# Router order, output products by column parity and an earlier side input in a two-layer encoder kernel

## The reference

```python
# layer 1's mixer: sliding-window attention, 16 query heads, 2 key heads, sinks
o = sliding_window_sink_attention(q, k, v, sinks)
return o @ w_out + b_out
...
# hierarchical_moe: router
g_logits = (t @ w_group) + b_group
g_prob = jax.nn.softmax(g_logits, axis=-1)
g_idx = jnp.argmax(g_logits, axis=-1)
g_w = jnp.max(g_prob, axis=-1)
e_logits = jnp.einsum('td,dge->tge', t, w_router) + b_router
e_sel = jnp.einsum('tge,tg->te', e_logits, g_onehot)
top_v, top_i = lax.top_k(e_sel, MOE_TOP_K)
top_w = jax.nn.softmax(top_v, axis=-1)
...
# every layer, at its end
gate = jax.nn.sigmoid(rms_norm(h, norm_ple[i]) @ ple_w_gate[i])
h = h + gate * (p[i] @ ple_w_proj[i])
```

## Time and profile before

| | us |
|---|---|
| median of 3 runs | 792.12 (791.20, 792.12, 795.34) |
| the profiled execution | 795.19, of which the span of the profile is 793.2 |

### The profile page before, as it was taken

The page is one execution under the profiler, slowest core; times in us unless marked ns, Lnnn a source line. Parts: engine busy times, 40 slices in busy tenths (PEclk is TensorE's granted clock), DMA queues, the critical chain, the costliest instruction groups (busy, mean ns, idle before and its releaser), DMA issues.

```text
span 793.2 us, 8335 instructions
## 1 busy us (share of the span) xinstructions
PE 747.0 (94%) x3180; PEld 346.5 (44%) x3180; DVE 278.6 (35%) x665; ACT 140.2 (18%) x344; POOL 29.9 (4%) x49
## 2 busy tenths in 40 slices
PE   6999999899999999989999979989999999988996
PEld 3445555474333333323445544476333333332444
DVE  0402331264246243323222564143533533232323
ACT  1100231222111111100311143212111111110031
POOL 0500000000000000000000020000000000000000
PEclk9999999999999999999999998989999999999999
DMA  9991521939999999999999670144999999999921
GB/s 336 325 356 55 212 88 71 391 140 358 423 421 420 421 421 421 421 421 420 385 292 299 267 299 1 53 159 164 409 421 421 422 419 421 421 421 422 404 94 54
DMA packets 49433, 245.24 MB, mean 309 GB/s; under 512 B 4080, under 2 KB 6480, under 8 KB 24816
## 3 DMA queue, kind: packets, MB, share of 16 engines
q1 hardware_dynamic: 48112, 242.15, 77.6%
q0 software_dynamic: 1104, 2.45, 0.9%
q10 hardware_dynamic: 176, 0.09, 0.0%
HBM read 243.61 MB, written 1.06 MB: 308 GB/s over the span
## 4 chain that ended last, share of the span: by engine, by line
PE 66%; DMA 15%; SPq 9%; DVE 6%; issue 3%; ACT 1%; POOLq 0%; POOL 0%; DVEq 0%; ACTq 0%
PE bank L611 28%; PE bank L849 14%; SPq L411 9%; PE bank L866 8%; DMA weights<-in_moe_w_up_dram 7%; DMA weights<-in_moe_w_down_dram 7%; PE bank L879 2%; PE bank L826 2%; PE bank L1026 1%; PE bank L595 1%; PE bank L787 1%; PE bank L858 1%; PE bank L650 1%; PE bank L670 1%; PE bank L794 1%
## 5 line engine op out<-in xcount | busy, mean ns | idle before, releaser
L611 PE MATMUL bank<-weights,normalised 128*128 128x512 f32 (+1 forms) x528 | 232.2, 594 | 10.1 <-DVE normalised L1963 4.0
L849 PE MATMUL bank<-weights,expert_rows 128*64 128x512 f32 x1024 | 228.1, 594 | 13.0 <-DMA weights<-in_moe_w_up_dram 12.9
L611 PEld LDWEIGHTS bank<-weights,normalised 128*128 128x128 f32 x528 | 100.2, 194 | 123.1 <-issue 114.5
L849 PEld LDWEIGHTS bank<-weights,expert_rows 128*64 128x64 f32 x1024 | 74.8, 137 | 155.3 <-issue 154.6
L866 PE MATMUL bank<-weights,hidden_turned 128*64 128x512 f32 x256 | 58.8, 598 | 1.3 <-DVE hidden_turned L1731 0.7
L866 PE MATMUL bank<-weights,hidden_turned_odd 128*64 128x512 f32 x256 | 58.8, 598 | 0.6 <-DMA weights<-in_moe_w_down_dram 0.6
L1317 ACT ACTIVATE gate_tanh<-bank 128x256 f32<-128x256 f32 x32 | 12.3, 385 | 206.0 <-PE bank L849 206.0
L1761 DVE TENSOR_TENSOR gather_onehots<-bank,expert_outputs 128x512 fp32r<-128x512 f32 x32 | 22.1, 691 | 54.5 <-ACT expert_outputs L1193 54.4
L1193 ACT ACTIVATE expert_outputs<-bank 128x512 fp32r<-128x512 f32 x32 | 19.1, 597 | 123.9 <-PE bank L866 123.9
L1731 DVE COPY hidden_turned<-bank 128x256 f32<-128x256 f32 x16 | 6.8, 425 | 85.1 <-PE bank L858 85.1
L1731 DVE COPY hidden_turned_odd<-bank 128x256 f32<-128x256 f32 x16 | 6.8, 425 | 78.4 <-PE bank L858 78.4
(11 more groups left out here) (249 smaller groups left out, 597.5 us busy)
## 6 DMA issues: line engine op xcount, KB each, us to landing
weights<-in_moe_w_gate_dram SPq DMA_DIRECT2D x64, 1024.0 KB, 18.6
weights<-in_moe_w_up_dram SPq DMA_DIRECT2D x64, 1024.0 KB, 20.4
weights<-in_moe_w_down_dram SPq DMA_DIRECT2D x64, 1024.0 KB, 22.3
weights<-in_even_w_in_dram SPq DMA_DIRECT2D x5, 2048.0 KB, 21.0
weights<-in_ple_w_gate_dram SPq DMA_DIRECT2D x4, 2048.0 KB, 30.9
weights<-in_even_w_out_dram SPq DMA_DIRECT2D x2, 2048.0 KB, 18.6
weights<-in_odd_w_qkv_dram SPq DMA_DIRECT2D x2, 2048.0 KB, 19.2
weights<-in_odd_w_out_dram SPq DMA_DIRECT2D x4, 1024.0 KB, 22.0
```

What stands on the lines that cost most here:

```text
L611: mm = pe.matmul(B[bank][:, 0:width], XT[:, k, tok(t)], w[:, k, :], start=(k == 0), stop=(k == KD - 1))
L849: mm = pe.matmul(bank[j * BLK:(j + 1) * BLK, :].rearrange("p (m f) -> p m f", m=2), rows[:, k, :], W[:, slots, a:a + FF // 2], start=(k == ...
```

## The change

1. On TensorE, layer 0's `experts` runs both halves of the last output product in one piece (layer 1's has one half left), and the logits of tile 0 are put on the two sides of the transposes of tile 1.
2. In the wait behind the logits, TensorE also turns `p[l]` (4 transposes to bank 3), and ScalarE copies it; `unread` goes from 12 and 9 to 10 and 8. GpSimd's queue fetches `p[l]` when layer 0's mixer inputs or layer 1's queries are turned. The work on `p` leaves the experts' steps.
3. On VectorE, the operations that lead only to the gates' weights (six behind `chosen`) move behind the gather's first copies; ScalarE's two exponentials move likewise. Two pairs of slot operations are interleaved with one wait fewer each. `rows_low(1)` is made in two parts, columns of blocks 0 to 3 ahead of the logits' wait and 4 to 7 behind the one-hots.
4. In layer 1, output products go by column parity (`out_part`): even blocks need VectorE's copy only, odd ones ScalarE's only. They begin earlier, VectorE's `mix_evac(0)` stands ahead of `max1(4)`, `turn_q(1)` ahead of `probs1(2)`, and one more half of products stands ahead of the router.
5. The bias is added to `H` by VectorE, between the updates of tile 0; GpSimd only fetches it.

The diff, cut to its core (left out: the moved SBUF buffers, the removed pieces of the experts' steps, and the same waits at other places):

```diff
+            def side_rows(l):
+
+                pool.wait_ge(*((sem("mix0_turned"), 2), (sem("q1_turned"), 4))[l])
+                pool.dma_start(PIN, p[l, 0].rearrange("(t p) d -> p t d", p=P)).then_inc(sem("p_landed"), 16)
...
             pool.tensor_tensor(BNR, BNE, HALF[:, 0:8], ALU.pow).then_inc(sem("gn_rstd"), 1)
+            side_rows(0)
             power(1)
...
             pool.dma_start(BO, bcast(odd_b_out)).then_inc(sem("bo_landed"), 16)
-            pool.wait_ge(sem("bo_landed"), 16)
-            for t in range(TT):
-                pool.wait_ge(sem("hT_ready"), 2 * (2 * 3 + t) + 2)
-                pool.wait_ge(sem("squares_ready"), 2 * 3 + t + 1)
-                pool.tensor_tensor(H[:, t, :], H[:, t, :], BO, ALU.add).then_inc(sem("bo_added"), 1)
+            side_rows(1)
...
-                for k in range(4 * half, 4 * half + 4):
+                for k in range(half, KD, 2) if n in (U_OUT1, U_OUT1 + 1) else range(4 * half, 4 * half + 4):
...
-                        pe.matmul(B[3][:, 0:P], ident, ident, start=True, stop=True)
-
-                project_rows(out, 1, 2, done)
+                        pe.matmul(B[4][:, 0:P], ident, ident, start=True, stop=True)
+
+                if l == 0:
+                    project_rows(out, 1, 2, done)
                 transposes(kn, 0, (4, 5))
-                project_part(out + 1, 1, 3, 0, done)
+                if l == 0:
+                    project_rows(out + 1, 1, 3, done)
+                else:
+                    project_part(out + 1, 1, 3, 1, done)
                 if l == 0:
                     pe.wait_ge(sem("small_landed"), 15 * 16)
                 logits(0, 0)
+                transposes(kn, 1, (6, 7))
                 logits(0, 1)
-                project_part(out + 1, 1, 3, 1, done)
-                transposes(kn, 1, (6, 7))
                 logits(1, 0)
                 logits(1, 1).then_inc(sem("logits_ready"), 1)
-                unread(12)
+                pe.wait_ge(sem("p_landed"), 16 * (l + 1))
+                pe.wait_ge(sem("h_updates"), h_done(kn - 1, 1))
+                for k in range(2):
+                    for t in range(TT):
+                        mm = pe.transpose(B[3][:, k * SEQ + t * P:k * SEQ + (t + 1) * P], PIN[:, t, k * P:(k + 1) * P], ident)
+                mm.then_inc(sem("pT_ready"), 1)
+                unread(10)
...
-                unread(9)
+                unread(8)
 
                 def gathered(group, t):
 
                     if group == 0:
                         pe.wait_ge(sem("onehots_ready"), 2 * l + t + 1)
-                        pe.wait_ge(sem("hs_low"), 2 * l + t + 1)
+                        if t == 0:
+                            pe.wait_ge(sem("pT_copied"), l + 1)
+                    if group == 0 or t == 1:
+                        pe.wait_ge(sem("hs_low"), 3 * l + 1 + t * (group + 1))
                     for k in range(4 * group, 4 * group + 4):
...
+            def out_part(c, t, bank, half):
+
+                pe.wait_ge(sem("mix1T_by_act" if half else "mix1T_by_dve"), t + 1)
+                project_part(U_OUT1 + c, t, bank, half, "out1_ready")
...
@@ -1143,29 +1148,30 @@
             probs1(1)
             scores1(3)
             values1(1)
+            turn_q(1, (6, 7))
             probs1(2)
-            turn_q(1, (6, 7))
             values1(2)
             probs1(3)
             scores1(4)
             scores1(5)
+            out_part(0, 0, 0, 0)
             values1(3)
-            mixed(0)
-            project_part(U_OUT1, 0, 0, 0, "out1_ready")
             probs1(4)
             scores1(6)
-            project_part(U_OUT1, 0, 0, 1, "out1_ready")
+            out_part(0, 0, 0, 1)
             values1(4)
             probs1(5)
             scores1(7)
-            project_part(U_OUT1 + 1, 0, 1, 0, "out1_ready")
+            out_part(1, 0, 1, 0)
             values1(5)
             probs1(6)
-            project_part(U_OUT1 + 1, 0, 1, 1, "out1_ready")
+            out_part(1, 0, 1, 1)
             values1(6)
             probs1(7)
+            out_part(0, 1, 2, 0)
             values1(7)
-            mixed(1)
+            out_part(1, 1, 3, 0)
+            out_part(0, 1, 2, 1)
             experts(1, U_MOE1)
...
+                act.wait_ge(sem("pT_ready"), l + 1)
+                copy(PINT.rearrange("p k s -> p (k s)"), B[3][:, :]).then_inc(sem("pT_copied"), 1)
+
                 def rows(e, off=None, part=slice(0, KD), done="xe_ready"):
...
+                    if half == 0:
+                        act.wait_ge(sem("g_below_max"), l + 1)
+                        act.activation(RT[:, 20:28], RT[:, 20:28], ACT.Exp).then_inc(sem("g_exp"), 1)
+                        act.wait_ge(sem("second_below_first"), l + 1)
+                        act.activation(RT[:, 84:86], RT[:, 84:86], ACT.Exp).then_inc(sem("second_exp"), 1)
...
                             add_rows(t, half, 2 * t + half)
                     mean_square(kn, t)
                     xt_evac(kn, t, 4 + 2 * t)
-                    if t == 0:
-                        rows_low(t)
+                    rows_low(t, 0, KD if t == 0 else 4)
                 t3 = lambda a, n: RT[:, a:a + 2 * n].rearrange("p (t n) -> p t n", t=TT)
...
                 picked(100, 2.0, ALU.is_lt).then_inc(sem("chosen"), 1)
                 picked(180, 0.0, ALU.is_equal)
                 then(picked(212, 1.0, ALU.is_equal))
-                dve.tensor_tensor(GB, LG, wide(GX, 4), ALU.subtract).then_inc(sem("g_below_max"), 1)
-                then(dve.tensor_tensor(SLT, O1, LE, ALU.mult))
-                then(dve.tensor_reduce(M1, SLT, AX.X, ALU.add))
-                then(dve.tensor_tensor(SLT, O2, LE, ALU.mult))
-                then(dve.tensor_reduce(M2, SLT, AX.X, ALU.add))
-                dve.tensor_tensor(SEC, M2, M1, ALU.subtract).then_inc(sem("second_below_first"), 1)
 
                 dve.wait_ge(sem("counts_ready"), l + 1)
                 then(dve.tensor_copy(CNT, B[2][:, 0:NE]))
...
-                then(dve.tensor_tensor(O1, O1, SLT, ALU.mult))
-                then(dve.tensor_reduce(S1, O1, AX.X, ALU.add))
-                then(dve.tensor_tensor(O2, O2, SLT, ALU.mult))
-                then(dve.tensor_reduce(S2, O2, AX.X, ALU.add))
+                dve.tensor_tensor(ORD, O1, SLT, ALU.mult)
+                then(dve.tensor_tensor(SLT2, O2, SLT, ALU.mult))
+                dve.tensor_reduce(S1, ORD, AX.X, ALU.add)
+                then(dve.tensor_reduce(S2, SLT2, AX.X, ALU.add))
                 dve.wait_ge(sem("iota_ready"), l + 1)
...
                 dve.tensor_copy(TBL[0:1, 0:NE], OFW[one]).then_inc(sem("table_ready"), 1)
-                rows_low(1)
+                rows_low(1, 4, KD)
+
+                def rows_evac(k):
+
+                    dve.wait_ge(sem("rows_ready"), 8 * l + k + 1)
+                    dve.tensor_scalar(XS[:, k, :], B[k][:, :], NW[:, kn, k:k + 1], None, ALU.mult).then_inc(sem("rows_by_dve"), 1)
+
+                rows_evac(1)
+                rows_evac(3)
+                dve.tensor_tensor(GB, LG, wide(GX, 4), ALU.subtract).then_inc(sem("g_below_max"), 1)
+                then(dve.tensor_tensor(SLT, O1, LE, ALU.mult))
+                then(dve.tensor_reduce(M1, SLT, AX.X, ALU.add))
+                then(dve.tensor_tensor(SLT, O2, LE, ALU.mult))
+                then(dve.tensor_reduce(M2, SLT, AX.X, ALU.add))
+                dve.tensor_tensor(SEC, M2, M1, ALU.subtract).then_inc(sem("second_below_first"), 1)
                 dve.wait_ge(sem("g_exp"), l + 1)
...
             normalise1(2)
             turned_q(1, 6)
             normalise1(3)
+            mix_evac(0)
             max1(4)
-            mix_evac(0)
             max1(5)
             normalise1(4)
             normalise1(5)
@@ -1997,11 +2008,18 @@
             normalise1(6)
             max1(7)
             normalise1(7)
-            dve.wait_ge(sem("bo_added"), 1)
-            for half in range(2):
-                dve.wait_ge(sem("out1_ready"), half + 1)
-                add_rows(0, half, half)
             mix_evac(1)
+            dve.wait_ge(sem("out1_ready"), 1)
+            add_rows(0, 0, 0)
+            dve.wait_ge(sem("bo_landed"), 16)
+            dve.wait_ge(sem("h_updates"), h_done(3, 0) - 1)
+            for t in range(TT):
+                dve.wait_ge(sem("hT_ready"), 2 * (2 * 3 + t) + 2)
+                dve.wait_ge(sem("squares_ready"), 2 * 3 + t + 1)
+                i = dve.tensor_tensor(H[:, t, :], H[:, t, :], BO, ALU.add)
+            then(i)
+            dve.wait_ge(sem("out1_ready"), 2)
+            add_rows(0, 1, 1)
```

53 lines of the change are left out of this document (16 added, 37 removed).

## The result

| | us |
|---|---|
| changed kernel, median of 4 executions | 780.57 (777.31, 779.64, 781.49, 783.00) |
| kernel before, same chip, median | 791.89 |
| ratio, 95% interval | 0.985 (0.982 to 0.988) |
| profiled execution, changed | 779.64, span 777.8 |

The change makes the kernel 1.5% faster; the forecast was 779.3. The profiled executions lie 795.19 - 779.64 = 15.55 us apart, the medians 11.3, because the profiled execution of before stood at the top of its range (791.2 to 795.3): its router of layer 1 had the half clock.

The account below looks back on a forecast made before the run. Expert-weight loads were taken to bound the kernel, restarting only when `first_rows(0)` has run. Savings of 8.5 (attention), 4.0 and 2.75 (routers of layers 1 and 0) and 0.6 (`p`), 15.9 us, gave 779.3; range 777 to 782, 8-in-10 range 776 to 785.5.

Parts of the forecast that it names:

- PEclk is 0.50 behind the logits: Both routers: TensorE's clock at half speed behind the logits, named as a sign that would make the prediction wrong.
- attention 8.5: Layer 1's attention: pause and half clock 6.7, tile 1's waits 1.4, earlier wait 0.4; together 8.5 us saved.
- moved logits of layer 1, 1.0: Layer 1's router: tile 0's logits fill waits behind the last product, 1.7 us less a new 0.7 wait; gain 1.0.
- layer 1's router behind it: Layer 1, rest of the router's 4.0 us: logits at full clock, earlier counts, fewer slot waits, gather without its wait.
- layer 0's router: Layer 0: 1.5 us up to the choice, 0.6 counts, 0.2 slot operations, 0.45 gather; together 2.75 us saved.
- `p`: Fetching its 256 KB outside the full stretch of loads, at 421 GB/s, saves 0.6 us for both layers.
- The terms 6.7 and 1.4: Layer 1's attention: 6.7 us from the first output product's pause and half clock, 1.4 from tile 1's two waits.
- the 0.4 for the waits ahead of them: Layer 1's attention: `turn_q(1)` put into the 1.59 us wait ahead of `probs1(2)`, counted as 0.4 us saved.
- The weaker attention: Rival: layer 1's attention gains only its pause, other waits replace the rest; 3 to 5 us less gain, chance 0.08.
- VectorE reads them at the 0.75 ... if the clock is full: Routers: VectorE reads the counts 0.75 us after its first pick; saves 0.6 us in layer 0, 1.15 in layer 1.
- the rival of half clock: Rival: the new router runs at half clock, costing 3.6 us per router; 783 for one, 786.5 for both; chance 0.2.
- 0.6 + 0.2 + 0.45 - 0.2: Router behind the transposes: earlier counts 0.6, fewer slot waits 0.2, gather without wait 0.45, less 0.2 for a later choice.

Follow-up runs that it names:

- changed_again: The changed kernel itself, run again unaltered for comparison and scatter; median 780.12 us, ratio 0.984 to the kernel before.
- router_only: The changed kernel with parts 4 and 5 undone (attention and bias as before); median 788.99 us, ratio 0.993 to the kernel before.
- bias_gpsimd: The changed kernel with the bias added by GpSimd again, all orders as in the change; median 783.46 us, ratio 0.989 to the kernel before.
- rows_later: The changed kernel with layer 1's low part of tile 0 moved behind the update of tile 1; median 777.68 us, ratio 0.982 to the kernel before.
- unread_none: The changed kernel without its 18 unread matmuls in each layer; median 785.12 us, ratio 0.990 to the kernel before.

## Why the prediction was right, and where not

The time (780.6 for 779.3), the order of the terms and most signs named for the trace came as written. Two did not: the counts are read 1.37 and 1.61 us after the first pick (0.8 forecast), and PEclk is 0.50 behind the logits, which the prediction itself had named as what would make it wrong. By stretches, of the profiled executions:

| | forecast | measured |
|---|---|---|
| attention 8.5 and moved logits of layer 1, 1.0 | 9.5 | 8.8 and 1.1 (A: 9.9) |
| layer 1's router behind it | 3.0 | 2.7 (R1) |
| layer 0's router | 2.75 | 2.4 |
| `p` | 0.6 | 0 |
| what no term is about | 0 | 0.5 |
| sum | 15.9 | 15.5 |

Layer 0's 2.4 is 175.25 - 172.55 = 2.7 less the 0.3 by which the changed program was already ahead at layer 0's first transposes. That 0.3, E0, E1, the stretch behind them and what lies outside the span are the 0.5. The sum comes within 0.4 us in part by luck: `p` and the half clock took away what the attention, the gather and that 0.5 brought beyond the forecast. In medians the change is worth 11.3, not 15.9. The prediction had foreseen the direction: a run of before without the half clock starts lower and gains less.

The attention. The pause of 3.97 and the half clock behind it went, as written, and the cause of the slow operations was GpSimd's addition. Either remedy helps: without the addition A falls by 5.5, and with the parity order the addition is largely covered. The terms 6.7 and 1.4 hold to 0.1; the 0.4 for the waits ahead of them was 0.6 (1.59 and 0.35 us before, 0.57 and 0.73 after). The weaker attention, 3 to 5 us less, didn't come.

The routers. The step that failed is "VectorE reads them at the 0.75 ... if the clock is full". It wasn't: the rival of half clock, to which I gave 0.2, was there in both routers, in a milder form than I priced. In the mild form it cost 17.8 - 17.0 = 0.8 each, not 3.6; in the strong form it costs 2.4. The rival's price took the whole stretch at 0.50, unread matmuls and logits, as in layer 1 before. Counting the six kernels whose router is that of the changed kernel (changed, changed_again, router_only, bias_gpsimd, rows_later and its repeat), the 12 routers show the full clock 3 times, the mild form 6 times and the strong one 3 times. Their mean extra is (6 x 0.8 + 3 x 2.4) / 12 = 1.0 us. At the full clock the new router is 18.4 - 17.0 = 1.4 us shorter than the old one behind the transposes (0.9 to 1.1 where both have the mild or both the strong fall), and I had forecast 0.6 + 0.2 + 0.45 - 0.2 = 1.05 there. The term that was too small is the gather: from its start to `first_rows(0)` it is 175.25 - 168.31 = 6.94 us before and 172.55 - 166.37 = 6.18 with the change, 0.76 for 0.45: beside the wait of 0.40, eight entries by themselves take 2.35 us, and a third of the piece of 24 takes 2.08. In layer 0 of bias_gpsimd, at the full clock, the counts are read 0.85 us after the first pick (0.75 forecast). So part of the mild form's 0.8 hid in my sum behind a router that gains more than I counted.

`p`. The term of 0.6 is wrong: it priced 256 KB at the 421 GB/s of the full stretch, so that 256 KB fewer in it would shorten it. E0 and E1 don't depend on where `p` is fetched, within the 0.5 us by which they vary anyway. Why the 256 KB don't show in them stays open.

The fact that the loads don't begin again before `first_rows(0)` carried the whole sum, and it held: E0 and E1 stay between 207.2 and 207.7 in every kernel but unread_none's 208.3, so all that is saved ahead of them arrives at the end. The profiled executions can be added up that way: unread_none is 2.53 + 4.01 + 0.98 - 0.31 (R0, R1, E1, E0) over the changed kernel, which gives 786.85; it ran in 786.86. Why its E1 is 0.98 longer isn't known.

## What to carry to other kernels

Where a small VectorE operation takes ten times its usual time, look for a large elementwise operation of GpSimd at the same moment, and who waits behind the small one; move that work to VectorE, under a product (here 1.2 us for each addition on VectorE, 2.3 on GpSimd). Compare profiled executions in stretches between two TensorE instructions: at a like clock they repeat to some hundredths of a us, where single executions lie up to 6 us apart. Fill a wait of TensorE with work it has to do anyway, but don't count on the clock there: price the router at each clock that its rows show, with a chance for each. And look for the clock in more than one execution of the kernel before: that it fell in layer 1 alone, and strongly, was one execution's.

## What the runs showed that I had not expected

The granted clock falls to 0.50 while TensorE is busy without a pause: 2.00 of 2.00 us from 514 to 516 us. What stood before the fall in layer 1 were 12 logits matmuls of 20 columns (24 entries) and the four transposes of `p`; in layer 0 it fell in the last of the logits. In the same program it falls within the logits in one execution or router, behind them in another, and not at all in a third. The Trainium skill ("TensorE: Matmul & The Clock Gate", "Part 1: The HAM clock gate") has the clock follow how busy the engine was; a wait adds to it here, too (unread_none, whose gathers run partly at 0.50).

GpSimd's addition of 128x1024 holds up VectorE's operation on 128x4 with two SBUF inputs: 0.16 us alone, 1.62 to 2.27 beside it, in all three kernels that have the addition there (before, router_only, bias_gpsimd). The small operation isn't slow, it ends with the addition: in bias_gpsimd the second addition ends at 467.44 + 4.65 = 472.09 us and VectorE's second operation at 469.84 + 2.27 = 472.11, and before at 476.44 and 476.46. So what it costs is what is left of the addition when it starts. Whether GpSimd is held up as well, no run shows: its additions take 2.33 us each in all three. VectorE's reduction from PSUM beside it is not touched: 0.68 us in bias_gpsimd.
